# Recurrence of an encoder layer: values centred when they are turned, norms per token on eight columns, keys turned ahead of the grams

## The reference, cut to what matters

```python
kk = (k * k_k).reshape(B, T, H, N)
kk = kk / maximum(sqrt(sum(kk * kk, axis=-1)), 1e-12)             # the key norm: per token and head
kd = k[:, :, None, :] * (1.0 + (a - 1.0) * k_a)
# per direction, token after token, S is 64 x 64 of a head:
#   S = S * w + (S a) b^T + v k^T ;  y = S r      with a = -kk, b = kk * iclr
y = ys[forward] + flip(ys[backward])
mu = mean(y, axis=-1); var = mean((y - mu) ** 2, axis=-1)          # over the 64 features of a head
yn = (y - mu) * rsqrt(var + GN_EPS) * ln_g + ln_b
bonus = sum(r * (kd[0] + kd[1]) * r_k, axis=-1) * v
out = (yn + bonus) * g
```

## Time and profile before

| | us |
|---|---|
| median of 3 runs | 1847.09 (1846.45 to 1847.62) |
| span of the profiled execution, first to last instruction | 1844.7 |
| PE busy in it | 1716.3 (93%) |
| DVE, ACT, POOL busy in it | 587.2, 352.7, 62.7 |

### The profile page before, as it was taken

The page is one execution under the profiler, slowest core; times in us unless marked ns, Lnnn a source line. Parts: engine busy times, 40 slices in busy tenths (PEclk is TensorE's granted clock), DMA queues, the critical chain, the costliest instruction groups (busy, mean ns, idle before and its releaser), DMA issues.

```text
span 1844.7 us, 37012 instructions
## 1 busy us (share of the span) xinstructions
PE 1716.3 (93%) x16070; PEld 1093.7 (59%) x16070; DVE 587.2 (32%) x1303; ACT 352.7 (19%) x945; POOL 62.7 (3%) x96
## 2 busy tenths in 40 slices
PE   6999999988989899998799999999999999999996
PEld 5888888867777445675455454444544454444543
DVE  2000333488886301021322322222232322222233
ACT  2112222156665201022200000000000000000002
POOL 1000000000000000002000000000000000000000
PEclk9999999999999999999899999999999999999999
DMA  9932335200000744326799999999999999999993
GB/s 323 183 111 92 117 111 179 102 4 4 4 4 4 283 174 170 126 114 244 270 421 430 426 430 428 432 429 433 428 431 432 428 432 429 433 428 430 430 425 147
DMA packets 96049, 503.63 MB, mean 273 GB/s; under 512 B 37820, under 2 KB 42320, under 8 KB 77248
## 3 DMA queue, kind: packets, MB, share of 16 engines
q1 hardware_dynamic: 91080, 488.17, 65.7%
q0 software_dynamic: 4608, 13.08, 2.4%
q10 hardware_dynamic: 248, 0.65, 0.1%
HBM read 511.29 MB, written 4.23 MB: 279 GB/s over the span
## 4 chain that ended last, share of the span: by engine, by line
PE 68%; DMA 22%; DVE 6%; issue 2%; ACT 1%; POOL 0%; DVEq 0%; SPq 0%; POOLq 0%; ACTq 0%
PE ps L1524 15%; DMA ring<-in_wd 9%; PE ps L2033 8%; PE ps L2155 8%; PE ps L2022 8%; PE ps L1849 6%; DMA rest<-in_wu 5%; DMA ring<-in_wu 5%; PE ps L2041 4%; DMA ring<-in_wg 2%; PE ps L1867 2%; PE ps L1918 2%; PE ps L1876 2%; DMA tmp<-in_bf 1%; PE ps L1935 1%
## 5 line engine op out<-in xcount | busy, mean ns | idle before, releaser
L1524 PE MATMUL ps<-wide,ring 128*128 128x256 f32 (+1 forms) x1280 | 282.2, 379 | 2.9 <-ACT wide L543 1.7
L1524 PEld LDWEIGHTS ps<-wide,ring 128*128 128x128 f32 (+1 forms) x1280 | 239.1, 187 | 48.4 <-issue 10.1
L1403 DVE TENSOR_TENSOR tokA<-tokA,ps 128x512 f32<-128x512 f32 x256 | 158.5, 682 | 101.4 <-PE ps L2041 101.4
L2033 PE MATMUL ps<-ring,wide 128*64 128x256 f32 x1512 | 171.3, 385 | 19.0 <-DMA ring<-in_wu 18.9
L2155 PE MATMUL ps<-ring,gg 128*64 128x512 f32 x768 | 175.4, 598 | 3.1 <-DMA ring<-in_wd 2.4
L2022 PE MATMUL ps<-ring,wide 128*64 128x256 f32 x1536 | 173.2, 383 | 2.5 <-DVE wide L1391 1.9
L1416 DVE SCALAR_TENSOR_TENSOR gg<-ps,tmp,gg 128x256 f32<-128x256 f32 x32 | 15.5, 484 | 476.8 <-PE ps L2033 476.8
L2033 PEld LDWEIGHTS ps<-ring,wide 128*64 128x64 f32 x1512 | 109.7, 139 | 78.7 <-DMA ring<-in_wu 24.9
L2022 PEld LDWEIGHTS ps<-ring,wide 128*64 128x64 f32 x1536 | 109.9, 138 | 57.1 <-DVE wide L1391 3.6
L2041 PE MATMUL ps<-wide,gg 64*128 64x512 f32 x512 | 135.3, 627 | 0.9 <-ACT wide L819 0.8
L2155 PEld LDWEIGHTS ps<-ring,gg 128*64 128x64 f32 x768 | 50.9, 136 | 121.5 <-issue 109.6
(11 more groups left out here) (366 smaller groups left out, 2053.9 us busy)
## 6 DMA issues: line engine op xcount, KB each, us to landing
ring<-in_wg SPq DMA_DIRECT2D x23, 4096.0 KB, 29.2
ring<-in_wu SPq DMA_DIRECT2D x23, 4096.0 KB, 30.2
ring<-in_wd SPq DMA_DIRECT2D x22, 4096.0 KB, 32.1
rest<-in_wd SPq DMA_DIRECT2D x8, 4096.0 KB, 30.3
ring<-in_w_in SPq DMA_DIRECT2D x7, 4096.0 KB, 15.1
rest<-in_wu SPq DMA_DIRECT2D x7, 4096.0 KB, 29.5
rest<-in_wg SPq DMA_DIRECT2D x7, 4096.0 KB, 30.2
ring<-in_w_out SPq DMA_DIRECT2D x4, 4096.0 KB, 17.3
```

The costliest lines, as they stand in the source:

```text
L1403: V.tensor_tensor(fin_part(t, h, n), fin_part(t, h, n), ps[:, banks[q][h], :], ALU.add).then_inc(S["added"], 1)
L1524: ins = mm(ps[0:rows_, m % 2, 0:T], lhs, hnT[:, k, :], start=k == 0, stop=k == KD - 1)
L2033: ins = mm(ps[CAP * h:CAP * h + CAP, 1, 0:T], xT[:, k, CAP * i:CAP * i + CAP], w[:, T * h:T * h + T], start=k == 0, stop=k == KD - 1)
```

## The change

Values: `v_turn` multiplies with `CE`, a new constant of 128x128, where it turned with the unit matrix. `CE` is the unit matrix less 1/64 within each head, so the turned values have mean zero per head, and so has y. The mean of y (L1680, L1834) and the deviation (L1066) are gone; `DSQ` is the square of `Yp` and is made at the end of a pair.

Norms: the sums over a head's features are taken per token. `norm_sums` on PE has the squares as its stationary operand and two columns of `BO` moving, so that 128 tokens (partitions) by 2 heads come out; two halves of tokens and two kinds (keys, heads) are the eight columns `nrm8`. Clamp, scale, square root and reciprocal work on these eight columns. `norms_spread` on PE then spreads the inverse norms back to feature-major, 128x256 per kind, by eight products of a column broadcast to 64 with the unit matrix. `norm_sums` stands behind step 7, `norms_spread` behind step 15; DVE now copies out steps 7 and 15, both before `norm_sums`' scaling and before the use of the spread norms.

Order: the eight transposes of `BKh` stand ahead of the grams, where two stood behind L1706 of each group. `bonus_terms` stands behind `quotients`, ahead of the wait for step 7. The copies to `RH` and `BNS` are POOL's. The products of the last pair stand inside the output projection: `norm_sums` ahead of its fourth product, `norms_spread` ahead of the tenth.

```diff
+CE = 1225
+NCST = 1353
+    c[:, CE:CE + P] = (i == j) - (i // CH == j // CH) / CH
-        Yp, DEV, VAR, DSQ, BNS = (nrm_[:, i] for i in range(5))
+        Yp, DEV, BTERM, DSQ, BNS = (nrm_[:, i] for i in range(5))
+        nrm8 = st[:, 48:56]
...
# POOL
-            for n in range(4 * CT):
-                pool.wait_ge(S["rw_mask"], n + 1)
-                pool.tensor_tensor(PRN[1][:, n % 4, :, 1, :], GB[:, n % 4, :, 0, :], eye, ALU.add).then_inc(S["rw_r1"], 1)
+            for p in range(CT):
+                for g in range(4):
+                    pool.wait_ge(S["rw_mask"], 4 * p + g + 1)
+                    pool.tensor_tensor(PRN[1][:, g, :, 1, :], GB[:, g, :, 0, :], eye, ALU.add).then_inc(S["rw_r1"], 1)
+                pool.tensor_copy(RH.rearrange("p (z b) t -> p z (b t)", z=2), AR[:, :, 1, :]).then_inc(S["rw_rhc"], 1)
+                if p:
+                    pool.wait_ge(S["rw_out"], p)
+                pool.tensor_copy(BNS, ew[:, BON]).then_inc(S["rw_bns"], 1)
...
# ACT
+            def norms(n, c):
+                act.wait_ge(S["rw_pv"], 2 * n + 1)
+                A(nrm8[:, c], nrm8[:, c], ACT.Sqrt).then_inc(S["rw_std"], 1)
-                    if n == 7:
+                    if n in (7, 15):
                         continue
-                    if n == 9:
-                        if not first:
-                            head_std(p - 1)
-                        if not last:
-                            key_norm(p + 1)
+                    if n == 8:
+                        norms(p, slice(4 if last else 0, 4 if first else 8))
...
# DVE
+            def norm_sums(keys_, heads):
+                if keys_:
+                    ins = V.tensor_scalar(nrm8[:, 0:4], ps[:, 7, T:T + 4], 1e-24, None, ALU.max)
+                if keys_ and heads:
+                    dc.add(ins)
+                if heads:
+                    ins = V.tensor_scalar(nrm8[:, 4:8], ps[:, 7, T + 4:T + 8], 1.0 / 64, GN_EPS, ALU.mult, ALU.add)
+                ins.then_inc(S["rw_pv"], 1)
+            def inverse_norms(n, c):
+                dve.wait_ge(S["rw_std"], n + 1)
+                V.reciprocal(nrm8[:, c], nrm8[:, c]).then_inc(S["rw_inv"], 1)
+            def normed_head(p, src):
+                dc.link(V.scalar_tensor_tensor(DEV, Yp, of(P_LG, p), src, ALU.mult, ALU.mult))
             def gated(p):
                 dc.sync()
-                dc.link(V.tensor_tensor(DEV, DEV, BNS, ALU.add))
+                dc.link(V.scalar_tensor_tensor(DEV, DEV, of(P_LB, p), BNS, ALU.add, ALU.add))
...
             def pair_(p, first, last, next_):
-                for g in range(3):
+                for g in range(4):
                     mask(p, g)
-                dve.wait_ge(S["rw_sums"], p + 1)
-                if not first:
-                    deviation(p - 1, ps[:, 6, T:2 * T])
-                if not last:
-                    square_sums(ps[:, 7, T:2 * T])
-                mask(p, 3)
-                dc.add(V.tensor_copy(RH.rearrange("p (z b) t -> p z (b t)", z=2), AR[:, :, 1, :]))
                 if not last:
                     for part in range(2):
                         scaled_keys(p + 1, part)
                 if next_:
                     quotients(p + 2)
+                if not last:
+                    bonus_terms(p + 1)
                 dve.wait_ge(S["rw_pt"], 24 * p + 8)
+                dc.add(V.tensor_copy(PRN[0][:, 3].rearrange("p e k n -> p e (k n)"), ps[:, 6:8, 0:3 * CH]))
+                norm_sums(not last, not first)
+                inverse_norms(p, which)
+                dve.wait_ge(S["rw_pt"], 24 * p + 16)
+                dc.add(V.tensor_copy(PRN[0][:, 3].rearrange("p e k n -> p e (k n)"), ps[:, 6:8, 0:3 * CH]))
                 if not first:
-                    variance(ps[:, 7, T:2 * T])
-                V.tensor_copy(PRN[0][:, 3].rearrange("p e k n -> p e (k n)"), ps[:, 6:8, 0:3 * CH]).then_inc(S["rw_pv"], 1)
-                if not first:
-                    inverse_std(p - 1)
-                    normed_head(p - 1)
+                    normed_head(p - 1, ps[:, 7, T:2 * T])
                 if not last:
-                    key_norms(p + 1)
+                    unit_keys(ps[:, 6, T:2 * T])
+                dc.sync()
+                dve.sem_inc(S["rw_pv"], 1)
+                if not last:
+                    dve.wait_ge(S["rw_rhc"], p + 1)
+                    products_ar(p + 1, 0)
                 if not first:
                     gated(p - 1)
-                dc.add(V.tensor_copy(BNS, ew[:, BON]))
                 if not last:
-                    unit_keys()
-                    bonus_terms(p + 1)
-                    products_ar(p + 1, 0)
                     products_bk(p + 1, 0)
                     products_out(0)
...
                 V.tensor_tensor(Yp[:, 0:T - CH], Yp[:, 0:T - CH], ps[:, 7, T:2 * T - CH], ALU.add).then_inc(S["rw_yp"], 1)
+                dve.wait_ge(S["rw_yp"], p + 1)
+                V.tensor_tensor(DSQ, Yp, Yp, ALU.mult).then_inc(S["rw_dsq"], 1)
                 if next_:
                     keys(p + 2)
...
# PE
-                    ins = tr(ps[:, 6 + b, P * c:P * c + P], rkv[:, 16 + 4 * (n // 2) + c, P * b:P * b + P], ident)
+                    ins = mm(ps[:, 6 + b, P * c:P * c + P], rkv[:, 16 + 4 * (n // 2) + c, P * b:P * b + P], cst[:, CE:CE + P], start=True, stop=True)
+            per_head = cst[:, BO:BO + P:CH]
+            def norm_sums(heads, keys_):
+                for wanted, sem_, src, o in ((keys_, "rw_sq", ew[:, SQ], T), (heads, "rw_dsq", DSQ, T + 4)):
+                    if wanted is not None:
+                        pe.wait_ge(S[sem_], wanted)
+                        for b in range(TB):
+                            ins = mm(ps[:, 7, o + 2 * b:o + 2 * b + 2], src[:, P * b:P * b + P], per_head, start=True, stop=True)
+                return ins
+            def norms_spread(n, keys_, heads):
+                pe.wait_ge(S["rw_inv"], n + 1)
+                for wanted, bank, o in ((keys_, 6, 0), (heads, 7, 4)):
+                    if wanted:
+                        for b in range(TB):
+                            for e in range(2):
+                                each = nrm8[:, o + 2 * b + e:o + 2 * b + e + 1].broadcast_to([P, CH])
+                                ins = mm(ps[CH * e:CH * e + CH, bank, T + P * b:T + P * b + P], each, ident, start=True, stop=True)
+                return ins
...
                 for g in range(4):
                     z, b = g // 2, g % 2
+                    for m in range(2):
+                        tr(ps[:, 2 * g, T + P * m:T + P * m + P], BKh[:, m, z, P * b:P * b + P], ident)
+                for g in range(4):
...
-                if not first:
-                    ins = mm(ps[:, 6, T:2 * T], ones2, Yp, start=True, stop=True)
-                if not last:
-                    pe.wait_ge(S["rw_sq"], p + 2)
-                    ins = mm(ps[:, 7, T:2 * T], ones2, ew[:, SQ], start=True, stop=True)
-                ins.then_inc(S["rw_sums"], 1)
...
-                    for m in range(2):
-                        ins = tr(ps[:, 2 * g, T + P * m:T + P * m + P], BKh[:, m, z, P * b:P * b + P], ident)
...
-                    if n == 7 and not first:
-                        pe.wait_ge(S["rw_dsq"], p)
-                        ins = mm(ps[:, 7, T:2 * T], ones2, DSQ, start=True, stop=True)
+                    if n == 7:
+                        ins = norm_sums(None if first else p, None if last else p + 2)
+                    if n == 15:
+                        ins = norms_spread(p, not last, not first)
...
-            pe.wait_ge(S["rw_yp"], CT)
-            mm(ps[:, 7, 0:T], ones2, Yp, start=True, stop=True).then_inc(S["rw_mu"], 1)
...
-                    if n == 0 and k == CT:
-                        pe.wait_ge(S["rw_dsq"], CT)
-                        mm(ps[:, 7, T:2 * T], ones2, DSQ, start=True, stop=True).then_inc(S["rw_var"], 1)
+                    if n == 0 and k == 3:
+                        norm_sums(CT, None).then_inc(S["rw_sums"], 1)
+                    if n == 0 and k == CT + 1:
+                        norms_spread(CT, False, True).then_inc(S["rw_bc"], 1)
```

More of the change, by code:

```diff
@@ L701, in _ @@
             pair_(CT - 1, False, True, False)
-            head_std(CT - 1)
+            norms(CT, slice(4, 8))
             squares(1, S["mem_in"], 16)
@@ L1101, in pair_ @@
             def pair_(p, first, last, next_):
-                for g in range(3):
+                which = slice(4 if last else 0, 4 if first else 8)
+                for g in range(4):
                     mask(p, g)
-                dve.wait_ge(S["rw_sums"], p + 1)
-                if not first:
-                    deviation(p - 1, ps[:, 6, T:2 * T])
-                if not last:
-                    square_sums(ps[:, 7, T:2 * T])
-                mask(p, 3)
-                dc.add(V.tensor_copy(RH.rearrange("p (z b) t -> p z (b t)", z=2), AR[:, :, 1, :]))
                 if not last:
@@ L1156, in pair_ @@
                     products_out(1)
```

(40 more changed lines are left out.)

53 lines of the change are left out of this document (17 added, 36 removed).

## The result

The changed kernel takes 1852.78 us (median of 9 runs, 1849.92 to 1854.83) where the kernel before takes 1847.74 on the same chips (9 runs, 1846.45 to 1849.50): 1.0027 times the time, 95% interval 1.0018 to 1.0035. It is slower, by 5 us; the forecast was 1836.8. Its profiled execution has a span of 1853.0 us, 8.3 more than the 1844.7 of the kernel before.

A forecast was written before the change was run, and what follows sets the result against it. No engine plainly bounds a pair; the chain runs over PE, then DVE, with PE's instruction supply close behind. 9.1 + 0.75 + 1.0 - 0.5 = 10.35 us off the 1844.7 span gave 1836.8 us, range 1827 to 1845.

The forecast's parts named there:

- the sum: Whole kernel: 9.1 us from seven pairs, 0.75 last pair, 1.0 end, less 0.5 ahead: 10.35 off the span of 1844.7.
- (c): In each pair, step 15, spread, copy and step 19 chain in series: 4.3 us slower, 1851.4; chance 0.06.
- The front of a pair: Grams and masks before the squaring: mean and deviation go, transposes move ahead; squaring starts 1.25 us earlier (0.7 to 1.6).
- The norms on PE: Within a pair: norm_sums 0.95 us in place of 0.63, norms_spread 1.1; together 1.4 more on PE, mostly filling stalls.
- DVE behind step 15: Copy, two operations, products: DVE ready for its four groups at 461.9, where it was 463.6; they follow PE's signals.
- The sum of the pair: PE becomes the bound; its mark moves from 463.34 to 462.6; a loop pair gains 1.3 us (1.0 to 1.9).
- The pair: Window of one loop pair: near 27.6 us, from 28.90; prediction wrong if over 28.3 or under 26.8.
- The fetch: PE's instructions come in blocks of some 260, each at least some 3.5 us; time saved inside one returns as stall.
- rival (a): Instruction supply is no limit in the pair; stalls vanish, each pair gains 2.5 us, about 1827.5; chance 0.18.
- one sign: In the profile after, PE's stalls by "issue" would be not smaller than 2 us a pair.
- The start: Ahead of the first pair: values turned by 32 passes instead of 16, costing some 0.5 us (0 to 1.9).
- The end: Last pair gains 0.75 us; in the output projection PE no longer waits for Yp, net 1.0.

The follow-up runs named there:

- the placed kernel: Changed kernel plus 34 idle semaphore increments on PE, 17 at each of two router waits, expert loop body at 5 in a packet: 1837.02 us, 0.9951 of the kernel before.
- 227: Loop body's place in its 256-instruction packet in the unpadded changed kernel (1852.78 us), and in the kernel before with 45 idle PE increments (1863.10 us, 1.0079).
- 243: Changed kernel with 16 idle increments on PE ahead of the experts, loop body beginning at 243 of a 256-instruction packet: 1859.45 us, 1.0070 of the kernel before.
- 10: Kernel before with 84 idle increments on PE ahead of the experts, loop body beginning at 10 of a packet: 1853.02 us, 1.0041 of the kernel before.
- 31: Changed kernel with 60 idle increments on PE ahead of the experts, loop body beginning at 31 of a packet: 1841.49 us, 0.9969 of the kernel before.
- the run of 14 increments: Kernel before with 14 idle increments on PE, 7 at each of two router waits, loop body at 196: 1847.68 us, beside 1848.13 unpadded.
- the expectation above: Written for the placed kernel with the BKh transposes put back behind L1706 of each group; that run measured 1843.97 us, 0.9993 of the kernel before.
- its padded forms: Kernel before with 14, 30, 45 or 84 idle increments on PE ahead of the experts: 1847.68, 1850.95, 1863.10 and 1853.02 us.
- the doubled products: The placed kernel with the first four products of a squaring step made twice in 16 steps, 256 more instructions a pair: 1863.38 us, 1.0098 of the kernel before.
- 212: Kernel before with 30 idle increments on PE ahead of the experts, loop body beginning at 212 of a packet: 1850.95 us, 1.0030 of the kernel before.

## Why the prediction was wrong, point by point

**The step that failed** is the sentence behind the sum: "All that follows hangs on the end of the recurrence and moves with it." It moved (the experts began 5.8 us earlier in the profiled execution, 11.2 in the placed kernel), but it did not stay the same length. I had counted the change's new instructions, 36 a pair, and priced them only where they are executed, at 0.5 us. That they push all code behind them along, and with it a loop of 1602 instructions that just fitted, I did not ask. It costs 14.1 us; without it the same code measures 1837.0, 8.9 us under the kernel before in the same runs, where the sum had 10.3. The page before held the two numbers that could have raised the question: PE with 16070 products and as many loads needs 126 packets of 256, and the queue for all engines had 97. So a good part of the code ran without being fetched, and what is kept must have a limit. No rival had this: (c), the slower one, sought the loss in the pair.

The Trainium skill (Runtime: NRT & Kernel Launch, Instruction fetch mechanics) gives PE a memory of 2048 instructions, filled in blocks of 256, and warns that a taken branch outside a window of two blocks makes a fetch. Seven blocks of body and one ahead of it would just be those 2048, an estimate from the page's figure. It agrees with the runs at 227 and 243 (long) and 5, 10, 31 (short), and not with the run of 14 increments, whose body touches eight blocks and is kept. The window of two doesn't agree: the kernel before jumps back over 1602 instructions in 0.25 us and no packet comes.

**The front of a pair**: right. The squaring begins 446.70 - 441.01 = 5.7 us into the pair, by the rows below, where it began 7.1 in the earlier trace rows: 1.4, with 1.25 forecast. But which part of it brings the gain I had split wrongly: the expectation above puts the order at 0.3, and it is worth 0.9 by the runs (6.95 us in eight pairs), 0.8 by PE's waits for the masks (4.8 us in six).

The chain of the changed kernel through the pair 440.95 to 468.74 (start, us, engine, tile, line, count):

```profile
441.01 1.02 PE ps L1687 x8
442.04 1.91 PE ps L1697 x64
...
446.70 0.23 PE ps L1733 x8
...
450.54 0.98 PE ps L1662 x8
...
455.41 1.02 PE ps L1672 x15
456.43 0.61 issue
457.04 0.28 PE ps L1672
...
459.89 0.87 issue
460.77 0.21 PE ps L1753
...
463.20 0.63 PE ps L1779 x2
...
464.44 0.42 DVE tokA L1033
464.86 0.19 DVE ring L1138
465.06 0.20 DVE ring L1140
465.48 0.43 DVE tmp L1147
```

**The norms on PE**: right. `norm_sums` (L1662) takes 0.98 (0.95 forecast), `norms_spread` (L1672) 1.02 for 15 of its 16 passes (1.1 for all). The spread of step 15 is through at 457.3, 16.4 us into the pair; forecast 456.6 - 440.06 = 16.5.

**DVE behind step 15**: the time right, the role wrong in part. DVE's timeline there:

```profile
452.82 0.20 DVE L1073 RECIPROCAL st<-st 128x8 f32<-128x8 f32 x1 [0.56 <-ACT st L637]
...
457.35 0.56 DVE L1114 COPY ring<-ps 128x384 f32<-128x384 f32 x1 [4.32 <-PE ps L1672]
...
462.42 0.76 DVE L1054 TENSOR_TENSOR ring<-ring,exps 128x256 f32<-128x256 f32 x2
463.09 0.28 DVE L1138 TENSOR_TENSOR ring<-ring,ps 128x128 f32<-128x128 f32 x1
```

The reciprocal of eight columns takes 0.20 as put, and DVE then stands 4.3 us for PE. It reaches its four groups 22.1 us into the pair (461.9 - 440.06 = 21.8 forecast). But there L1138 follows DVE's own product without a wait, where I had said it would wait for PE; and between the groups lies a half of `bonus_terms` (L1033, 0.42), which I had left out of them. The chain holds two stalls by "issue", 0.61 at the spread and 0.87 behind step 19.

The sum of the pair said that PE's mark, the end of the last L1762 (L1775 now), would move from 23.3 us into the pair to 22.5, and that PE would then be the bound. In this pair it stands at 464.21, 23.2: the earlier start of the squaring went into the norms, the stalls and the wait at step 19. Over the five loop pairs the mark moved by 1.1 us in the mean. What ends a pair is the output that the copy of y waits for, and DVE's last group beside it:

```profile
464.92 0.33 PE L1792 MATMUL ps<-ring,wide 64*64 64x64 f32 x5
```

```profile
464.97 0.27 DVE L1140 SCALAR_TENSOR_TENSOR ring<-cst_sb,exps,ps 128x64 f32<-128x64 f32 x1
```

Here both are through at 465.25, and the copy of y starts at 465.48. In the mean of the five loop pairs DVE was 0.2 us later than PE before (later in four of the five), and PE is 0.2 later than DVE now (in pairs 1, 4 and 5, where the copy waits 1.0 us for it in all). So PE did become the bound, but by a little and not in each pair, and the chain, which ends on DVE in this one, shows the other half of a tie.

**The pair**: right. From the start of one pair to the next it is 27.79 us here; the first four from pair 1 on have 27.81, 27.80, 27.89 and 27.40. 27.6 was forecast, 26.8 to 28.3 allowed. Pair 5 has 28.49 (29.55 before) and pair 6 28.43, both beyond 28.3, and pair 6 gained nothing (28.41 before); the first was 0.5 longer, the last, up to the output projection, 2.8 shorter. The placed kernel, with the same code, has 27.25, 27.13, 27.48, 27.27, 26.93 and 27.62. The six traces with this code in the pairs have means of 27.2 to 27.9 over the five loop pairs, so the 0.7 us between these two is no finding; nor is the 0.5 of the first pair, which takes 31.3 to 33.3 us in the traces of the kernel before and its padded forms.

**The fetch**: right, and rival (a) with it wrong, though one sign missed. Instruction packets stay at 3.9 us in the mean after (36 in 139.39 us) against 4.0 before, the pauses stand at the first instruction of a packet, and the doubled products show the limit. PE's stalls by "issue" were to be no smaller than 2 us a pair; all such rows of the five loop pairs add up to 7.7 us, 1.5 a pair, where they were 13.3 before, 2.7 a pair. New work took the place of nearly half of them. A new wait at step 19 was put at up to 0.5: the longest is 0.4. The first wait of the spread for DVE did not come.

**The start**: wrong in cause. It is 2.0 us late, not 0.5; but the 32 passes account for 0.7 at most and the waits, moved ahead of the transposes, cost nothing in the end, since the first pair waits for DVE and ACT. **The end** gained more than forecast: last pair and end together 2.8 (29.95 us from the last pair's first gram, 584.76, to the output projection before; 27.19 from its first transpose after), 3.2 in the placed kernel, forecast 1.75. The prediction's 28.26 for the last pair is counted from 585.92, 1.2 us behind its first gram.

**What stays open.** Why at 212 only every second branch is long; where between 196 and 212 the edge is, and what rule puts it some instructions into the eighth packet. Fetch and half clock come together in every kernel here. The busy times bound the clock's part: PE is busy 2.1 us longer in the changed kernel's experts (897.2 for 895.1) and idle 12.1 longer, so most of the 14.1 us is standing still.

## What to carry to other kernels

Compare the time behind a change as well, stage by stage, before asking why the changed stage behaves so: here the changed part did as it was told and an untouched loop paid. Where a kernel has a loop whose body is large for its engine (here some 1600 instructions of PE), count how the body lies against packets of 256 (the pauses by "issue" in dense code show where a packet begins), and after each change of the code ahead look at the instruction queue inside the loop: packets in a loop that had none, and stalls by "issue" at the branch, are the sign. A few idle instructions in a place where the engine waits then give the time back (34 of them here, and the ratio goes from 1.0027 to 0.9951, 14 us).

## What the runs showed of the hardware

- A loop of PE of 1602 instructions in seven packets, or 10 instructions into an eighth, ran from what was already loaded: no instruction packet in 600 us, 0.25 us for the branch. When it reached 41 into the eighth, it was fetched again at each of five branches: 6.0 to 6.4 us for the branch and some 3.6 soon after, with 10 to 14 us at 1.2 GHz. It costs 14.1 to 14.3 us of 955, in both kernels; 20 at 57 into the eighth.
- In the dense small products of the recurrence PE had one packet of 256 instructions for each 3.66 us, and 256 more instructions whose own work is an estimated 1.8 us took 3.3. Its long pauses there stand at the first instruction of a packet, 14 of 15 in the kernel before.
- An increment of a semaphore on PE's own queue takes 0.15 us: 84 of them made the experts begin 7.6 us later, and 34 at two waits left the whole gain in place.
